# Another order of VectorE's work around three LayerNorms of a two-block transformer kernel

## The reference, cut to what matters

```python
for l in range(2):
    ada = c_act @ w_ada[l] + b_ada[l]
    sh1, sc1, gt1, sh2, sc2, gt2 = split(ada, 6)
    u = x * (1.0 + sc1) + sh1
    y = mixer(u, ...)                       # ends in merged @ w_out[l]
    x = layer_norm(DN_ALPHA * x + (1.0 + gt1) * y, ln_mix_g[l], ln_mix_b[l])
    u = x * (1.0 + sc2) + sh2
    h = jnp.square(jax.nn.relu(u @ w_up[l])) @ w_down[l]
    x = layer_norm(DN_ALPHA * x + (1.0 + gt2) * h, ln_ffn_g[l], ln_ffn_b[l])
```

## Time and profile before

| what | value |
| --- | --- |
| timed runs | 1985.27, 1981.39, 1981.9 us; median 1981.9 us |
| profiled execution: span from the first to the last instruction | 1979.4 us (of its own time the views give the span alone) |
| TensorE matmul busy | 1812.8 us, 92% |
| TensorE weight loads busy | 1423.8 us, 72% |
| VectorE busy | 1306.6 us, 66% |
| ScalarE busy | 872.4 us, 44% |
| GpSimd busy | 53.4 us, 3% |
| mean granted clock of TensorE | 0.971 |
| DMA | 345.90 MB, mean 175 GB/s |

### The profile page before, as it was taken

How to read it: one execution, slowest core, us unless ns; L and a number is a source line. 1 busy time by engine, 2 the same in 40 slices (tenths; PEclk the granted TensorE clock), 3 DMA queues, 4 the chain that set the end, 5 groups by cost and what they waited for, 6 DMA issues and landing times.

```text
span 1979.4 us, 26135 instructions
## 1 busy us (share of the span) xinstructions
PE 1812.8 (92%) x8350; PEld 1423.8 (72%) x8350; DVE 1306.6 (66%) x2017; ACT 872.4 (44%) x1462; POOL 53.4 (3%) x116
## 2 busy tenths in 40 slices
PE   4799998899898998999489999999999999999997
PEld 1565676677575576787389777778879977778886
DVE  3669987556768987555545688765555568875554
ACT  0343433343343334444155566444436556644443
POOL 0000000000100001000000000000000000000000
PEclk9899999999999999999799999999999999999999
DMA  7565446666385555565366533455565653346553
GB/s 245 179 221 170 149 154 239 203 222 213 108 267 168 171 170 171 199 204 171 106 196 190 170 127 99 147 186 177 179 212 170 193 171 128 107 139 191 180 175 122
DMA packets 210879, 345.90 MB, mean 175 GB/s; under 512 B 20105, under 2 KB 95799, under 8 KB 210533
## 3 DMA queue, kind: packets, MB, share of 16 engines
q1 hardware_dynamic: 208758, 337.79, 52.3%
q0 software_dynamic: 2032, 6.97, 1.3%
HBM read 343.62 MB, written 1.07 MB: 174 GB/s over the span
## 4 chain that ended last, share of the span: by engine, by line
issue 50%; POOLq 1%; POOL 0%; DVE 0%
POOLq L1627 0%; POOLq L1616 0%; POOLq L1625 0%; POOL x_rstd L1628 0%; DVE x_res L1852 0%; POOL gates L1610 0%; POOL x_rstd L1629 0%; POOL sub_rstd L1617 0%; POOL x_squares L1624 0%; POOLq L1635 0%; POOLq L1450 0%; POOL lat_rstd L1617 0%; POOLq L374 0%
## 5 line engine op out<-in xcount | busy, mean ns | idle before, releaser
L126 DVE TENSOR_TENSOR w_lo_b<-w_raw_b,w_hi_b 128x1024 fp32r<-128x1024 f32 (+3 forms) x336 | 362.0, 1100 | 188.7 <-ACT w_hi_b L120 187.0
L120 ACT CAST w_hi_b<-w_raw_b 128x1024 fp32r<-128x1024 f32 (+3 forms) x336 | 313.3, 950 | 165.9 <-PE prod_b L142 78.5
L140 PE MATMUL prod_b<-w_hi_b,hT_hi 128*128 128x512 f32 (+1 forms) x912 | 342.2, 375 | 12.3 <-ACT proj_b L1657 6.9
L120 ACT CAST w_hi_a<-w_raw_a 128x1024 fp32r<-128x1024 f32 x232 | 240.8, 1049 | 227.5 <-PE acc_a L142 104.0
L142 PE MATMUL prod_b<-w_hi_b,hT_lo 128*128 128x512 f32 (+1 forms) x912 | 334.1, 366 | 0.0
L141 PE MATMUL prod_b<-w_lo_b,hT_hi 128*128 128x512 f32 (+1 forms) x912 | 332.9, 365 | 0.0
L126 DVE TENSOR_TENSOR w_lo_a<-w_raw_a,w_hi_a 128x1024 fp32r<-128x1024 f32 x232 | 277.1, 1220 | 75.2 <-ACT w_hi_a L120 72.3
L140 PE MATMUL prod_a<-w_hi_a,uT_hi 128*128 128x512 f32 x592 | 249.3, 421 | 38.1 <-DVE w_lo_a L126 26.3
L142 PE MATMUL prod_a<-w_hi_a,uT_lo 128*128 128x512 f32 x592 | 240.8, 407 | 0.0
L141 PE MATMUL prod_a<-w_lo_a,uT_hi 128*128 128x512 f32 x592 | 240.7, 407 | 0.0
L140 PEld LDWEIGHTS prod_b<-w_hi_b,hT_hi 128*128 128x128 f32 x912 | 172.6, 189 | 44.0 <-DVE w_lo_b L126 11.9
(11 more groups left out here) (314 smaller groups left out, 2444.5 us busy)
## 6 DMA issues: line engine op xcount, KB each, us to landing
w_raw_a<-in_w_in_dram SPq DMA_DIRECT2D x72, 512.0 KB, 4.2
w_raw_b<-in_w_in_dram SPq DMA_DIRECT2D x192, 172.0 KB, 2.4
ada_raw<-in_w_ada_dram SPq DMA_DIRECT2D x64, 512.0 KB, 6.5
w_raw_a<-in_w_up_dram SPq DMA_DIRECT2D x64, 512.0 KB, 4.7
w_raw_a<-in_w_down_dram SPq DMA_DIRECT2D x64, 512.0 KB, 5.5
w_raw_b<-in_w_gate_dram SPq DMA_DIRECT2D x96, 256.0 KB, 2.9
w_raw_b<-in_w_ffn_gate_dram SPq DMA_DIRECT2D x88, 256.0 KB, 3.5
w_raw_b<-in_w_ffn_up_dram SPq DMA_DIRECT2D x88, 256.0 KB, 4.2
```

The lines of the kernel that those rows point to most:

```text
L120: act.copy(self.hi[:, s, 0:cols], self.raw[:, s, 0:cols]).then_inc(self.hi_done, 1)
L126: dve.tensor_tensor(self.lo[:, s, 0:cols], self.raw[:, s, 0:cols], self.hi[:, s, 0:cols].bitcast(F32), ALU.subtract).then_inc(self.lo_done, 1)
L140: pe.matmul(out, a_hi, w_hi, start=first and c == 0, stop=False)
```

## The change

It reorders VectorE's list at the three places. No instruction is added, removed or altered, and no other engine's list changes.

```diff
@@ between the layers
                     last_residual(0, 0)
                     last_residual(0, 1)
-                    split(layer(l, 0, G1), 1)
-                    last_residual(1, 0)
+                    split(layer(l, 0, G1), 2)
                     next_u(0, 0)
                     next_u(0, 1)
+                    split(layer(l, 2, G1), 1)
                     take_u_lo(0)
+                    last_residual(1, 0)
+                    take_u_lo(1)
                     last_residual(1, 1)
-                    split(layer(l, 1, G1), 2)
-                    take_u_lo(1)
+                    split(layer(l, 3, G1), 1)
                     next_u(1, 0)
-                    split(layer(l, 3, G1), 1)
+                    next_u(1, 1)
                     take_u_lo(2)
-                    next_u(1, 1)
                     take_u_lo(3)
@@ behind the mixer, both layers
                 mix_residual(0, 0)
                 mix_residual(0, 1)
-                split(layer(l, at + 8, G1), 1)
-                mix_residual(1, 0)
+                split(layer(l, at + 8, G1), 2)
                 next_u2(0, 0)
                 next_u2(0, 1)
+                split(layer(l, at + 10, G1), 1)
                 take_u2_lo(0)
+                mix_residual(1, 0)
+                take_u2_lo(1)
                 mix_residual(1, 1)
-                split(layer(l, at + 9, G1), 2)
-                take_u2_lo(1)
+                split(layer(l, at + 11, G1), 1)
                 next_u2(1, 0)
-                split(layer(l, at + 11, G1), 1)
+                next_u2(1, 1)
                 take_u2_lo(2)
-                next_u2(1, 1)
                 take_u2_lo(3)
```

## The result

| what | before | changed |
| --- | --- | --- |
| timed runs, median | 1981.64 us (4 runs, 1980.8 to 1985.27) | 2000.57 us (4 runs, 1997.37 to 2005.47) |
| ratio | | 1.008, 95% interval 1.0055 to 1.0105 |
| both measured again beside the experiments | 1987.55 us | 2003.27 us, ratio 1.0093 (1.0067 to 1.0119) |
| span of the profiled execution | 1979.4 us | 1995.4 us (of a run of 1997.37 us) |
| mean granted clock | 0.971 | 0.969 |

The forecast was 1999.2 us, 17.3 us more than before. The ratio of 1.008 is 15.9 us on 1981.64, with 10.9 to 20.8 as its interval. The two medians themselves differ by 18.9 us, which lies inside it. The ratios given here are not quotients of the medians shown beside them; the two differ by up to 0.0016.

The account below looks back on a forecast made before the run. TensorE was taken to bound the kernel wherever it is fed (matmuls fill 92% of the span). Place 1 5.8, place 2 5.8 and place 3 5.7 to 5.8 give 17.3 us, hence 1999.2 us; range 1991 to 2005.

Parts of the forecast that it names:

- Its mechanism: At each place, VectorE's wait for take 1 delays token tile 1's norm and turn 2, leaving a TensorE gap.
- Steps 1 to 3, the start: Start of place 1: turn 0 0.75 us earlier, but low part 2 ahead of take 0 makes group 0 0.39 late.
- Step 6: GpSimd's second pair at place 1: takes 2.09 us, or 2.54 at the other end; root ready at 296.49 or 296.94.
- Step 4, the wait at take 1: VectorE at place 1: stands still 2.15 us ahead of take 1, and everything behind it waits too.
- Step 5: Place 1: take 1 at 291.21 against 291.17; residual (1, 1) from 291.81 instead of 286.52; mean and variance 2.30 later.
- my short end of 2.09: GpSimd's second pair at place 1: the shorter duration assumed, 2.09 us from start to end, against 2.54.
- Step 7, the gap: TensorE ahead of turn 2 at place 1: turn 2 at 298.23 against 293.41, a new gap of about 4.7 us.
- Step 8, the clock: Behind the new gap at place 1: clock 0.50, token tile 1's group 0 at 301.85 against 296.04, 5.8 us late.
- its high end: Per place: longer GpSimd pair adds 0.45, lower clock into token tile 1's first group 1.0; 7.2 late, 21.7 in all.
- Its remark on the first gap of place 1: Place 1, before the change: first gap brought back the lower clock, so group 0 took 2.40 us against 1.50 for group 2.
- that rival: Behind places 1 to 3: later waits absorb 3 to 4 us a place, 6 to 8 left, 1989 us; chance 0.10.

Follow-up runs that it names:

- low part 1 away from the root: Changed kernel with low part 1 moved behind the two normed halves of token tile 0, VectorE idle during GpSimd's root: 2004.59 us, ratio 1.0106.

## Why the prediction was right

Its mechanism held at all three places, and its total lies inside the measured interval. That the total came so near is partly luck. The places cost 18.7 us by the trace, not 17.3; the stretches that the change doesn't touch were 2.7 us shorter in this execution, and so the spans differ by 16.0. Inside a place two steps were off with opposite signs: the start and take 1 by 0.7 us, GpSimd's second pair by 0.3 the other way.

- **Steps 1 to 3, the start.** Turn 0 was to be 0.75 earlier and is 0.19 earlier behind the mean (4.96 against 5.15). I had taken the first root at its old 0.56; low part 1, moved beside it, made it 1.47, and VectorE waited 0.46 us for it. Step 6 had weighed just this effect, for the second root only. So group 0 was 0.95 late (8.23 against 7.28), not 0.39. The experiment with low part 1 away from the root shows the cause of the long root.
- **Step 4, the wait at take 1.** 2.15 predicted, 2.25 measured, and the experiment that puts take 1 behind residual (1, 1) shows that it carries about three quarters of the loss.
- **Step 5.** Take 1 was to come as before, at 11.79 behind the mean by my sum; it came at 12.52. Of the 0.73, 0.56 are the late start of group 0. Group 0 took 0.30 longer, 2.70 (286.07 to 288.77) and not 2.40: here the clock had fallen by its start, in the kernel before it fell 0.3 us behind it. From turn 1 to take 1 it took 0.13 less.
- **Step 6.** The second pair took 1.75 from start to end, below my short end of 2.09, because the addition took 1.06 instead of 1.21 and the root, 0.55 with nothing beside it, started 0.14 behind its end, not 0.32. The rule cited from the Trainium skill ("GPSIMD Engine Reference", section "1. Specifications") would have given the right sign at both roots. The trace agrees with it where GpSimd's instruction starts while a low part runs (1.47); a root that started just ahead of one took 0.55 and wasn't slowed (the last section).
- **Step 7, the gap.** 4.7 predicted; 4.21, 3.95 and 4.21 measured. Turn 2 came 5.2 us later behind the mean at places 1 and 3 (19.15 and 19.18 against 13.99), against 4.8 predicted, and 4.55 later at place 2 (19.10 against 14.55), against 4.3.
- **Step 8, the clock.** Token tile 1's first group came 6.0, 5.4 and 5.75 us late at the three places (22.63, 22.09 and 22.36 against 16.62, 16.66 and 16.61 behind the mean): 17.2 in all against 17.3. At place 1 the lower clock lasted into that group and through it, which the forecast had only in its high end; hence 7.2 for this place and a sum of 18.7. This is the term that the forecast had too small. Its remark on the first gap of place 1 needs a limit: what brought the lower clock to group 0 there is two pauses of 1.88 and 1.48 us with turn 0 between them, not one long gap like the new one.
- **What is behind.** No delay was absorbed: the 4.44 us gap behind place 1 is 4.44 in the changed kernel, shifted as a whole, and that rival is out. TensorE's row there:

```profile
325.25 0.77 PE L140 MATMUL acc_a<-w_hi_a,aT_hi 128*128 128x512 f32 x1 [4.44 <-DVE w_lo_a L126]
```

What stays open: when the clock falls and rises around such a gap. The windows below are of the changed kernel, with the columns as above: one in the gap of place 1, one behind the clock's fall there, and three from turn 2 on at place 2.

```profile
292.80:296.20 3.40, 0.00 (x0) 0.00 (x0) 2.46 (x5) 0.00 (x0) 1.60 (x2) 1.00 0.11 22
296.60:303.00 6.40, 6.01 (x16) 4.77 (x17) 2.44 (x4) 0.60 (x1) 0.00 (x0) 0.50 0.65 227
538.05:538.45 0.40, 0.40 (x4) 0.40 (x5) 0.40 (x1) 0.00 (x0) 0.00 (x0) 1.00 1.03 394
538.85:541.85 3.00, 3.00 (x8) 2.30 (x7) 1.22 (x2) 0.48 (x1) 0.00 (x0) 0.50 0.16 62
543.00:544.40 1.40, 1.40 (x10) 1.22 (x9) 0.25 (x1) 0.88 (x2) 0.00 (x0) 1.00 0.00 0
```

At place 1 the clock was up for most of the gap, fell between 296.20 and 296.60, just ahead of turn 2, and stayed down to 6.0 us behind the start of turn 2. At place 2 it was still up through the gap and turn 2 (538.04), fell behind it, and was up again 3.9 us behind turn 2's start; at place 3 it was up again 2.7 us behind it. The same kernel run again had the long form at place 3 as well. No run shows why. And the 1.66 us in the rest of the span I haven't traced.

## What to carry to other kernels

In an in-order list, look behind each wait: ask what stands behind it that others need, and let it go first if it is ready. Here one take ahead of one residual was about three quarters of the loss. Getting the first tile ready early was worth nothing here, by 0.2 us or by 1.1, since VectorE's whole list was due by a later step; count the work up to that step and the pauses in it. And where two engines disturb each other, a step that is moved carries its disturbance along: price its old neighbour and its new one.

## What the runs showed of the hardware

- Whether GpSimd's small instructions are slow depends on what runs on VectorE when they start. Started inside a low part (both inputs in SBUF), they end only with it or after it: in the changed kernel the addition from 278.13 ends at 279.34, the low part at 279.30; the root from 279.66 ends at 281.13, the low part at 280.70. Without one the addition took 0.19 and the root 0.55 to 0.56. A root that started 0.06 ahead of a low part (293.62 and 293.68, take 1 behind residual (1, 1)) took 0.55 all the same, and that low part its usual 1.22. The kernel before has the same in the earlier trace rows: its root of 0.56 started at 281.24, ahead of an instruction of VectorE that also reads both inputs from SBUF:

```profile
281.56 0.69 DVE L1009 SCALAR_TENSOR_TENSOR x_res<-x_res,proj 128x512 f32<-128x512 f32 x1
```

  In this block all ten traces follow one pattern. The addition took 0.18 to 0.19 and the root 0.55 to 0.57, also where VectorE read PSUM or had a single SBUF input at their start; behind a low part already running they took 1.05 to 1.21 and 1.34 to 1.47, and behind a step of the norm (lines 771 and 773) already running the root took 0.88 to 0.89 where that step was 512 columns wide, and 1.58 where it was 1024. That VectorE holds a path to SBUF for the length of its instruction would explain it; this was only argued, no run was made for it.
- Matmuls whose results nobody needs, put into a gap, kept the clock at its upper level behind it: in the gap of 4.2 us they took turn 2 to turn 3 from 6.04 to 3.65 us, though the total didn't show it; in seven gaps of a stage they made the kernel 3.8 us faster (0.8 to 6.7).
